# Splitting a half matrix and its copies differently at the start of each expert stage of a two-layer decoder kernel

## The reference

```
def hier_moe(h, ...):
    ...                                   # top-1 group, top-2 experts in it: 32 experts, 256 tokens
    def expert_block(args):
        tok, e = args
        xb = x2[tok]
        hid = jax.nn.silu(xb @ w_gate[e]) * (xb @ w_up[e])
        return hid @ w_down[e]
```

## Time and profile before

| | us |
|---|---|
| time before, median of 3 runs (1109.8 to 1110.1) | 1109.93 |
| time of the profiled execution | 1110.2 |
| its span | 1108.4 |
| PE busy | 903.1 (81%) |
| DVE busy | 416.5 (38%) |
| ACT busy | 243.8 (22%) |
| mean DMA rate over the span | 398 GB/s |

### The profile page before, as it was taken

How to read it: one execution, slowest core, us unless ns; L and a number is a source line. 1 busy time by engine, 2 the same in 40 slices (tenths; PEclk the granted TensorE clock), 3 DMA queues, 4 the chain that set the end, 5 groups by cost and what they waited for, 6 DMA issues and landing times.

```text
span 1108.4 us, 21929 instructions
## 1 busy us (share of the span) xinstructions
PE 903.1 (81%) x9146; PEld 593.1 (54%) x9146; DVE 416.5 (38%) x1006; ACT 243.8 (22%) x622; POOL 41.9 (4%) x65
## 2 busy tenths in 40 slices
PE   9999989978685867677799998999676858585875
PEld 6877745645353535353488676656443525353532
DVE  6888433332222222222288665333221222222222
ACT  5567311100000000000265863111010000000012
POOL 0012200000000000000000312000000000000000
PEclk9999989989887888788999999999887978888899
DMA  9898999999999999999998668999999999999995
GB/s 353 251 402 334 358 410 429 427 429 429 429 428 428 429 427 429 429 429 428 408 386 345 233 270 356 427 427 429 427 430 429 427 428 430 427 428 430 429 426 234
DMA packets 56577, 440.73 MB, mean 398 GB/s; under 512 B 12113, under 2 KB 12625, under 8 KB 31058
## 3 DMA queue, kind: packets, MB, share of 16 engines
q1 hardware_dynamic: 56240, 440.02, 95.7%
q10 hardware_dynamic: 290, 0.07, 0.0%
HBM read 439.03 MB, written 1.05 MB: 397 GB/s over the span
## 4 chain that ended last, share of the span: by engine, by line
PE 49%; DMA 35%; SPq 5%; another core or an unknown queue 3%; DVE 3%; ACT 2%; issue 1%; POOL 0%; POOLq 0%; ACTq 0%; DVEq 0%
DMA ring<-in_w_expert_up 27%; PE banks L1138 14%; DMA ring<-in_w_expert_down 7%; PE banks L1166 6%; PE banks L1106 6%; PE banks L1179 3%; PE banks L1015 3%; PE banks L1019 3%; PE banks L1016 3%; SPq L524 2%; SPq L472 1%; PE banks L1232 1%; PE banks L1234 1%; PE banks L1233 1%
## 5 line engine op out<-in xcount | busy, mean ns | idle before, releaser
L1138 PE MATMUL banks<-ring,scratch 128*32 128x256 f32 x4096 | 287.2, 443 | 129.2 <-DMA ring<-in_w_expert_up 128.8
L1138 PEld LDWEIGHTS banks<-ring,scratch 128*32 128x32 f32 x4096 | 150.3, 127 | 260.2 <-issue 122.2
L1665 DVE TENSOR_SCALAR scratch<-scratch 128x128 f32<-128x128 f32 x64 | 14.5, 227 | 510.3 <-ACT scratch L779 507.6
L1166 PE MATMUL banks<-ring,xn 128*32 128x256 f32 x2048 | 137.0, 410 | 7.7 <-DMA ring<-in_w_expert_down 7.5
L778 ACT ACTIVATE scratch<-banks 128x128 f32<-128x128 f32 x64 | 17.8, 278 | 511.1 <-PE banks L1138 499.7
L1106 PEld LDWEIGHTS banks<-scratch,h 128*128 128x128 f32 x448 | 107.7, 334 | 5.8 <-issue 5.8
L1106 PE MATMUL banks<-scratch,h 128*128 128x128 f32 x448 | 110.4, 405 | 0.0
L1179 PE MATMUL banks<-xn 32*128 32x256 f32 x1024 | 74.8, 403 | 36.5 <-ACT xn L788 36.5
L1166 PEld LDWEIGHTS banks<-ring,xn 128*32 128x32 f32 x2048 | 63.6, 116 | 60.0 <-issue 23.1
L1179 PEld LDWEIGHTS banks<-xn 32*128 32x128 f32 x1024 | 50.3, 186 | 67.8 <-issue 67.7
L1440 DVE SCALAR_TENSOR_TENSOR split<-ring,gains,split 128x512 fp32r<-128x512 f32 x96 | 69.7, 765 | 24.1 <-ACT split L826 23.3
(11 more groups left out here) (177 smaller groups left out, 792.9 us busy)
## 6 DMA issues: line engine op xcount, KB each, us to landing
ring<-in_w_expert_gate SPq DMA_DIRECT2D x62, 2048.0 KB, 45.5
ring<-in_w_expert_up SPq DMA_DIRECT2D x61, 2048.0 KB, 48.8
ring<-in_w_expert_down SPq DMA_DIRECT2D x56, 2048.0 KB, 47.5
ring<-in_w_in_even SPq DMA_DIRECT2D x5, 2048.0 KB, 17.8
ring<-in_w_expert_down SPq DMA_DIRECT2D x10, 1024.0 KB, 10.0
ring<-in_w_in_odd SPq DMA_DIRECT2D x5, 2048.0 KB, 19.7
ring<-in_w_expert_up SPq DMA_DIRECT2D x6, 1024.0 KB, 11.0
ring<-in_w_out_even SPq DMA_DIRECT2D x2, 2048.0 KB, 9.0
```

Of the source, the lines that this page charges most:

```text
L1138: last = pe.matmul(psum[6][32 * j:32 * j + 32, 0:2 * P].rearrange("p (a s) -> p a s", a=2), xT[:, c, SLOTS * k:SLOTS * k + SLOTS], ring[:, ...
L1166: last = pe.matmul(psum[4][32 * q:32 * q + 32, 0:QUARTER], hidT[k][:, 32 * j:32 * j + 32], ring[:, DOWN_AT[k], D * j + QUARTER * q:D * j + ...
```

## The change

The half matrix is loaded into `stage` in three pieces, each as soon as the gather has read its columns: 1024 columns after the second place count (`placed`), 512 after the first half of the second gather, 512 after the second half. The first half of up is loaded in two quarters, after 2 and after 4 of the 8 row chunks. On DVE, `count_rounds` becomes `choice_shares` (the inverse gate sums, where it was) and `count_tokens` (the number of rounds, now behind `hidden` of expert 0), and `copy_stage` moves into the first `hidden`, between the swish and the transposition. POOL waits for the second up quarter's mark in place of the first half's, which is the same chunk.

```diff
-FIRST_PIECES = (4, 8)
-EXTRA_LOADS = [{0: 2 * len(FIRST_PIECES) - 3, GE - 1: l} for l in range(LAYERS)]
+FIRST_PIECES = (2, 4, 8)
+STAGED = 4
+EXTRA_LOADS = [{0: len(FIRST_PIECES) - 1, GE - 1: l} for l in range(LAYERS)]
...
+STAGE_PIECES = (1024, 1536, 2048)
...
-                sp.wait_ge(gathered[l], 2)
-                sp.dma_start(stage, gate_rows[row][:, 0:512 * FIRST_PIECES[0]]).then_inc(stage_arrived, 16)
+                for begin, end in zip((0,) + STAGE_PIECES, STAGE_PIECES):
+                    if begin == 0:
+                        sp.wait_ge(placed, (T + 1) * l + T)
+                    else:
+                        sp.wait_ge(gathered[l], STAGE_PIECES.index(end))
+                    sp.dma_start(stage[:, begin:end], gate_rows[row][:, begin:end]).then_inc(stage_arrived, 16)
...
-                        if i or n:
+                        if n or end > STAGED:
...
-                pool.wait_ge(piece_used, (len(FIRST_PIECES) - 1) * l + 1)
-                pool.wait_ge(stage_arrived, 16 * (l + 1))
+                pool.wait_ge(piece_used, (len(FIRST_PIECES) - 1) * (l + 1))
+                pool.wait_ge(stage_arrived, 16 * len(STAGE_PIECES) * (l + 1))
...
-            def count_rounds(l, link):
+            def choice_shares(l, link):
...
                 dve.reciprocal(by, by).then_inc(first_gates, 1)
+
+            def count_tokens(l, link):
...
-                dve.wait_ge(stage_arrived, 16 * (l + 1))
+                dve.wait_ge(stage_arrived, 16 * len(STAGE_PIECES) * (l + 1))
...
                 dve.tensor_tensor(hb, eb, gb[:, P:2 * P], ALU.mult).then_inc(hid_ready[l], 1)
+                if first:
+                    copy_stage(l)
                 dve.wait_ge(hid_ready[l], e + 1)
...
-                count_rounds(l, route_link)
-                dve.wait_ge(gate_steps, GATE_STEPS * (l + 1))
-                copy_stage(l)
+                choice_shares(l, route_link)
                 for k in range(AHEAD):
                     hidden(l, k, k, first=(k == 0), links=0)
+                    if k == 0:
+                        count_tokens(l, route_link)
+                        dve.wait_ge(gate_steps, GATE_STEPS * (l + 1))
                     gate_slots(l, k, k, k, links=SILU_LINKS)
```

## The result

The changed kernel takes 1111.75 us (median of 20 runs, 1109.0 to 1114.64), the kernel before 1109.87 us in the same comparison (20 runs, 1107.95 to 1111.86). The ratio is 1.0019, with a 95% interval of 1.0012 to 1.0027: 1.9 us slower, where 1.5 were forecast. Both kernels scatter by 4 to 5 us from run to run, so that a single profiled execution isn't a measurement of the difference. The one of the changed kernel took 1113.86 us (span 1112.1), 2.1 us above its median.

What follows compares the result with a forecast made beforehand. The weight stream was taken to bound the kernel, so only its stops at each stage's start count. Layer 0's +0.3 and layer 1's +1.2 gave +1.5 us, 1111.4 as median; range 1108.3 to 1113.4.

Steps and rivals of the forecast that it cites:

- What costs: At PE's entry into the loop: the moved count delays the number of rounds, and load, branch and entry move with it.
- How late: PE's load of the number and entry into the loop: 1.35 us later in layer 0, 1.4 in layer 1.
- The advance of the stream: At each stage's start: earlier small transfers put the stream ahead by 1.3 us in layer 0, 1.7 in layer 1.
- What it is worth: At expert 6's pair: the advance is worth 0 in layer 0 and at most 1.65 us in layer 1.
- Worth 0: Layer 0, expert 6's pair: the stream already runs dry there, so an earlier start only lengthens the stop at 157.
- 1.4 to 1.65: Saving in us from the earlier transfers over the whole kernel, if PE's times stayed.
- PE's clock: From loop entry to pair, 9.86 or 11.96 us by clock: layer 0 -0.7 to +1.35, layer 1 -0.25 to +1.85.
- the long stretch: PE at 1.2 GHz after the pause, as in layer 0 through 144 to 154; entry to pair then 11.96 us.
- rival 3: Both layers get the long slow stretch: 3.2 us slower, 1113.1; sign: layer 1's entry over 1.5 us later; chance 0.25.
- +0.3 and +1.2: Forecast slowdown in us from the later pair of expert 6: +0.3 in layer 0, +1.2 in layer 1.

Runs made afterwards that it cites:

- experiment 1: The changed kernel with the token count put back ahead of the first hidden; ratio to the kernel before 0.9983.
- experiment 2: The transfers of the change (stage pieces, up quarters) with DVE's order of the kernel before; ratio to the kernel before 0.9985.
- experiment 3: The kernel before with only DVE's new order (copy inside the first hidden, count behind it), transfers undivided; ratio 1.0035 to the kernel before.
- experiment 4: The changed kernel with the count moved on behind the hidden of expert 1; ratio to the kernel before 1.0065.
- experiment 9: The kernel before with six small idle products at the start of PE's program, nothing changed at the stages; ratio to the kernel before 1.0011.
- experiment 10: The changed kernel with the count inside the first hidden, between the swish and the copy; ratio to the kernel before 1.0009.
- experiment 7: The kernel of experiment 2 with three keep_warm calls (six matmuls in the trace) behind the sums; ratio to the kernel before 1.0013.
- experiment 8: The kernel of experiment 2 with up's half in one transfer again, stage pieces kept; ratio to the kernel before 1.0006.

## Why the prediction was right

**What costs: right.** The step that the forecast rested on, that PE's load, branch and entry follow the count, is shown from four sides: the count put first, made later, put between, and the branch taken away with the count left late. In these and the changed kernel a later entry goes with a higher ratio.

**How late: close.** Forecast were 1.35 and 1.4 us for the load, measured 1.6 and 1.5; for the entry 1.35 and 1.4, measured from the start of the first product 1.2 and 1.8 us. One part of the load's difference is visible: the first instruction of the swish takes 0.63 us beside POOL's copy, where it took 0.23.

**The advance of the stream: mis-sized.** The step "the stream is ahead by 0.58 MB = 1.3 us in layer 0 and 0.75 MB = 1.7 us in layer 1" assumed that the small pieces lose nothing. At the moment that it names, 5.4 us after the start of the first product, the windows give 0.10 and 0.40 MB, and after 10 us 0.30 and 0.21 MB, 0.7 and 0.5 us. The start of the pieces was as good as assumed; but the 4.4 us from 1.0 to 5.4 us ran at 230 and 256 GB/s, below the 331 and 296 of before, and the 9 us at 303 and 309, below 330 and 350. Whether the size of the transfers does that, or the smaller strips of each row that they move, or that less is issued ahead, no run tells apart.

**What it is worth: right in the sum, wrong for layer 0.** "Worth 0" in layer 0 was read from one execution, in which its pair was late because of the slow clock (12.0 us from the entry to the pair). In other executions it took 9.4 to 9.5 us (experiments 1 and 2), and then there is room. The gain of the transfers alone, 0.9985, is 1.7 us, about what the prediction's 1.4 to 1.65 said. That is luck in part: the prediction took all of it from layer 1, and by the bytes of the table it comes from both layers.

**PE's clock: both layers outside their bounds, the sum near by luck.** Layer 0's pair came 1.6 us sooner (forecast 0.7 sooner to 1.35 later), because its slow stretch ended by 151 and the way from the entry to the pair took only 9.2 us; layer 1's came 3.8 us later (forecast 1.4 to 3.5), with a chain of 11.8 us. For layer 1 the long stretch was the right choice. The profiled execution, 1113.86 us, is the forecast's rival 3 by its own sign: layer 1's entry is over 1.5 us later and the clock is at 1.2 GHz past 700. The median of the runs lies at the forecast sum. The shares of +0.3 and +1.2 for the layers are not borne out, and the parts were larger than forecast on both sides: the late count cost 4.0 us (from 0.9983 to 1.0019, with intervals of about 1 us on either side) where +1.5 and the 1.4 to 1.65 saved make some 3, and the earlier transfers with the count in front gave 1.9.

From the entry to the pair PE took 12.0, 9.2, 9.5, 9.4, 11.7, 9.4, 9.5 and 7.9 us in layer 0 (before, changed, experiments 1, 2, 3, 4, 9 and 10), and 9.9, 11.8, 9.8, 9.9, 10.1, 9.9 and 11.2 in layer 1 (the same without 9), with no stop of the kind of experiments 7 to 9 of over 0.5 us in between. The code of PE differs little among them. That may be behind the scatter of 4 to 5 us in both kernels; it was read from single profiles and not tested by itself.

**What stays open.** In the profiled executions the part from layer 1's first product to the end of the span grew by 3.5 us (429.5 to 432.9). The stream's 2.6 us around the pair less the 0.5 us of advance are 2.1 of them. The other 1.4 us lie in the last microseconds of the stream: its rate falls 2 us later than before, but its last bytes then take 3.1 us in place of 1.6, at 26 and 33 GB/s, until the last down product can go on. Windows of the kernel before and of the changed one:

```profile
1094.90:1096.50 1.60, 0.78 (x16) 0.18 (x12) 0.00 (x0) 0.00 (x0) 0.00 (x0) 1.00 0.10 33
```

```profile
1097.10:1100.20 3.10, 2.42 (x44) 0.97 (x40) 0.00 (x0) 0.37 (x1) 0.00 (x0) 1.00 0.08 26
```

Why the last bytes take longer is open. As this execution was 2.1 us above the median, it may be part of the scatter.

## What to carry to other kernels

An instruction that frees a sequencer's load and branch counts as work on the critical path, even when the engine behind it has several microseconds of matmuls queued: look up when the sequencer arrives (the register and branch instructions have source lines in the trace), not when the engine is idle. When the parts of a change pull in different directions, try them apart. Here the earlier transfers alone gave 0.9985, with the count put first 0.9983, both better than the kernel before and than all of it together. And where a loop is entered by a branch beside a busy stream of transfers, the place of the code itself can cost time, 1.2 us here by the ratio of experiment 9; a control with the same number of idle instructions put elsewhere tells that apart from the edit.

## What the runs showed of the hardware

- The branch on PE took 5.8 to 6.6 us in all eleven profiled executions that have it, beside a stream of 412 to 440 GB/s. In layer 1, PE could go past one place in the code only 12.2 to 13.0 us after the load of the number; where it got there sooner it stopped, for up to 3.65 us. 24 instructions at the other end of the program moved that stop by exactly 24 instructions.
- PE's sequencer loaded the number 7.0 us after the start of the first product, 0.9 us before the sums of layer 0 began in the kernel before, so it ran ahead by the sums and the last of the matmuls before them, more than 4 us of work.
- With pieces of 256 and 512 KB issued about 1 us apart, the 4.4 us from 1.0 to 5.4 us after the start of expert 0's product ran at 230 and 256 GB/s, where the kernel before, with pieces of 1 MB, had 331 and 296, with the DMA engines' busy share at 0.80 and 0.83 against 0.97 and 0.90. The Trainium skill (DMA: Bandwidth & Descriptors, Bandwidth) asks for transfers of 1 MiB or more; the trace agrees with the direction, though no run sets the size alone, and yet the small pieces came out ahead, because they could start sooner.
